# Seven block products for ten pairs of gate blocks, and 32x32 turns that go through device memory, in a two-layer gated mixer trunk

## What is computed

```
h = rms_norm(x, pre_g);  proj = h @ w_in           # w_in: 2048 x 24576
q_a k_a v_a z_a | u b c z | q_r k_r v_r z_r | g_a g_c g_r = split(proj)
o_a = dilated_attention(q_a, k_a, v_a) * silu(z_a) # 12 heads x 128
o_c = b * causal_conv3(c * u) * silu(z)            # 1536 channels
o_r = retention(rotary(q_r), rotary(k_r), v_r) * silu(z_r)
merged = sigmoid(g_a)*(o_a @ w_a) + sigmoid(g_c)*(o_c @ w_c) + sigmoid(g_r)*(o_r @ w_r)
x = x + rms_norm(merged @ w_out, post_g)
```

## Time and profile before

| | us |
|---|---|
| median of three runs (2746.15 to 2746.77) | 2746.62 |
| profiled execution, from first to last instruction | 2743.0 |
| time outside that span | 3.6 |
| PE busy | 2732.6 |
| DVE busy | 1924.2 |
| ACT busy | 1222.0 |
| POOL busy | 27.5 |

### The profile page before, as it was taken

One profiled execution on the slowest core, in us unless ns is written; L12 is line 12 of the kernel. 1 busy time (PEld: TensorE's weight loads), 2 busy tenths in 40 slices (PEclk: granted clock), 3 DMA queues, 4 the chain that ended last, 5 costly groups with the idle time before them and its releaser, 6 DMA issues.

```text
span 2743.0 us, 30433 instructions
## 1 busy us (share of the span) xinstructions
PE 2732.6 (100%) x12264; PEld 2268.3 (83%) x12264; DVE 1924.2 (70%) x2558; ACT 1222.0 (45%) x1404; POOL 27.5 (1%) x35
## 2 busy tenths in 40 slices
PE   9999999999999999999999999999999999999998
PEld 7888888888888888888878888888888888888887
DVE  6788744777655898858567887457676558977584
ACT  6454544444443334444454545444444433434443
POOL 0000000000000000000000000000000000000000
PEclk9999999999999999999999999999999999999999
DMA  9555566565555555556575555555656565555563
GB/s 333 184 172 196 170 200 194 190 199 188 196 195 190 184 184 176 182 195 221 180 238 175 184 190 179 197 188 187 202 193 198 188 197 177 191 171 182 199 215 138
DMA packets 264732, 529.10 MB, mean 193 GB/s; under 512 B 8464, under 2 KB 8848, under 8 KB 264336
## 3 DMA queue, kind: packets, MB, share of 16 engines
q1 hardware_dynamic: 260976, 517.50, 57.4%
q10 hardware_dynamic: 2608, 4.78, 0.5%
q0 software_dynamic: 1008, 4.87, 0.5%
HBM read 522.94 MB, written 4.19 MB: 192 GB/s over the span
## 4 chain that ended last, share of the span: by engine, by line
PE 99%; DVE 0%; issue 0%; ACT 0%; DVEq 0%; POOL 0%; POOLq 0%
PE ps L651 32%; PE ps L652 32%; PE ps L653 32%; PE ps L586 0%; PE ps L606 0%; PE ps L604 0%; PE ps L603 0%; PE ps L582 0%; PE ps L567 0%; PE ps L587 0%; PE ps L581 0%; PE ps L669 0%; DVE gates L1183 0%; DVE w_trail L913 0%; DVEq L231 0%
## 5 line engine op out<-in xcount | busy, mean ns | idle before, releaser
L913 DVE TENSOR_TENSOR w_trail<-raw,w_lead 128x1024 fp32r<-128x1024 f32 x973 | 1188.7, 1225 | 763.8 <-ACT w_lead L723 754.4
L723 ACT ACTIVATE w_lead<-raw 128x1024 fp32r<-128x1024 f32 x973 | 1028.3, 1060 | 1394.1 <-PE ps L653 1387.3
L651 PE MATMUL ps<-w_lead,hT_lead 128*128 128x512 f32 x3328 | 1299.1, 390 | 0.8 <-issue 0.4
L653 PE MATMUL ps<-w_lead,hT_trail 128*128 128x512 f32 x3328 | 1295.2, 389 | 0.0
L652 PE MATMUL ps<-w_trail,hT_lead 128*128 128x512 f32 x3328 | 1295.1, 389 | 0.0
L651 PEld LDWEIGHTS ps<-w_lead,hT_lead 128*128 128x128 f32 x3328 | 625.0, 188 | 131.1 <-issue 2.2
L653 PEld LDWEIGHTS ps<-w_lead,hT_trail 128*128 128x128 f32 x3328 | 624.9, 188 | 130.0
L652 PEld LDWEIGHTS ps<-w_trail,hT_lead 128*128 128x128 f32 x3328 | 625.1, 188 | 128.4
L651 PE MATMUL ps<-w_lead,oT_lead 128*128 128x512 f32 x576 | 224.3, 389 | 0.0
L653 PE MATMUL ps<-w_lead,oT_trail 128*128 128x512 f32 x576 | 224.1, 389 | 0.0
L652 PE MATMUL ps<-w_trail,oT_lead 128*128 128x512 f32 x576 | 224.1, 389 | 0.0
(11 more groups left out here) (102 smaller groups left out, 781.7 us busy)
## 6 DMA issues: line engine op xcount, KB each, us to landing
raw<-w_in SPq DMA_DIRECT2D x381, 1024.0 KB, 5.1
raw<-w_out SPq DMA_DIRECT2D x32, 1024.0 KB, 5.0
raw<-w_branch_a SPq DMA_DIRECT2D x24, 1024.0 KB, 5.0
raw<-w_branch_c SPq DMA_DIRECT2D x24, 1024.0 KB, 5.0
raw<-w_branch_r SPq DMA_DIRECT2D x24, 1024.0 KB, 5.0
raw<-w_in SPq DMA_DIRECT2D x5, 512.0 KB, 5.0
gates<-x SPq DMA_DIRECT2D x4, 512.0 KB, 13.5
post_gain<-post_norm_g POOLq DMA_DIRECT2D x2, 1024.0 KB, 8.2
```

The lines of the kernel that those rows point to most:

```text
L651: pe.matmul(acc, lead[:, k, tok(t)], wl, start=(k == 0), stop=False)
L653: last = pe.matmul(acc, trail[:, k, tok(t)], wl, start=False, stop=(k == BLOCKS[n][2] - 1))
L723: act.activation(w_lead[:, h % SPLIT_SLOTS, :], raw[:, i % RAW_SLOTS, part:part + HALF * COLS], ACT.Copy).then_inc(lead_ready, 1)
L913: dve.tensor_tensor(w_trail[:, s, :], raw[:, i % RAW_SLOTS, part:part + HALF * COLS], w_lead[:, s, :].bitcast(F32), ALU.subtract).then_inc ...
```

## The change

**Turns.** The evictions now write q, k, z and the conv product in an order cut by 32 columns (`quads`), and PE reads the weights of those blocks in that order (`columns`: runs of 32 elements). ACT sends the tile to a buffer in device memory (`send_away`, 512 KB) and starts four transfers that bring it back with its 32-row bands exchanged (`bring_back`, rows of 1 KB). Then two DVE transposes of all 128 partitions finish it (`turn_back`) where there were sixteen of 32 partitions. `probs` is turned as before. There are 24 such trips in a layer.

**Pairs.** For ten pairs of gate blocks (in each layer attention 2+3, conv 0+1 and 2+3, retention 0+1 and 2+3) the first eight slices of both blocks are multiplied as a 2x2 by 2x2 block product with seven products of four slices and one token tile instead of eight. A pair runs as 22 units in the order `PAIR_ORDER`; 14 of them are product units of 6 matmuls, 8 are plain units of 12. Four products need sums of weights: POOL adds a chunk from device memory onto a chunk in its raw slot by an accumulating transfer (`chunk_sum`, 1 MiB) once that chunk has been split for its earlier use. The left sides are formed once a layer (`form_work`). `p1`, `p6` and `p7` add up in one side bank; ACT copies the bank out after each (`pair_copy`), DVE forms differences (`pair_rest_of`), adds them at eviction, and ACT applies the sigmoid behind that.

**Conv's tail** runs gates 0 and 1, branches 0 and 1, gates 2 and 3, branches 2 and 3. `RAW_SLOTS` becomes 5, with slots given out by last use; `post_gain` shares the storage of `v_sb` and `q_sb`; constants are laid out for the new column order.

```
+PAIRED_GATES = {"attention": (2,), "conv": (0, 2), "retention": (0, 2)}
+PAIR_ORDER = ("p1", "q3", 0, 0, "q5", 0, 0, "p2", "p6", "p7", 1, 1, "q4", 1, 1)
+PAIR_CHUNK_ORDER = ((0, 0), (1, 1), (0, 2), (0, 3), (0, 1), (1, 2), (1, 3))
+SUM_AFTER = {"q5": "p1", "p7": "q3", "p6": "q5", "q4": "p6"}
...
 ACT_DUE = due({
-    "attention": [("exp", 4 * B + 1), ("out", 6 * B + 1)],
-    "conv": [("out", 4 * B + 6)],
-    "retention": [("square", 4 * B + 3), ("out", 5 * B + 3)]}, AHEAD)
+    "attention": [("q_away", 2 * B - 1), ("q_back", 2 * B + 1), ("k_away", 3 * B - 1), ("k_back", 3 * B + 1),
+                  ("exp", 4 * B + 1), ("z_away", 5 * B + 4), ("z_back", 5 * B + 6), ("out", 6 * B + 1)],
+    "conv": [("prod_away", 2 * B + 1), ("prod_back", 2 * B + 3), ("z_away", 4 * B + 1), ("z_back", 4 * B + 3),
+             ("out", 4 * B + 6)],
+    "retention": [("q_away", 2 * B + 1), ("q_back", 2 * B + 3), ("k_away", 3 * B + 1), ("k_back", 3 * B + 3),
+                  ("square", 4 * B + 3), ("z_away", 4 * B + 6), ("z_back", 4 * B + 8), ("out", 5 * B + 3)]}, AHEAD)
...
+PAIR_COPY_DUE = {UNIT_AT[kind, n, 1] + AHEAD: (kind, n) for n in PAIRS for kind in ("p1", "p6", "p7")}
+PAIR_REST_DUE = {UNIT_AT[kind, n, 1] + AHEAD + 1: (kind, n) for n in PAIRS for kind in ("p6", "p7")}
...
+            def chunk_sum(l, what, n):
...
+                wait(*split_done(l, UNIT_AT[SUM_AFTER[what], n, CHUNK // HALF - 1]))
+                at = l * tiles + row * CHUNK
+                pool.dma_start(raw[:, slot, :].rearrange("p (k n) -> p k n", k=CHUNK),
+                               weights[name][:, at:at + CHUNK, col:col + COLS],
+                               accum_op=ALU.add).then_inc(summed[SUMMED_FOR[what]], 16)
...
+            def product(l, h, what, n, part):
...
+                if part == 0:
+                    if what == "p1":
+                        pe.wait_ge(*side_bank_free(l, p_step))
+                    elif what == "q5":
+                        pe.wait_ge(*side_bank_free(l, q_step))
+                        pe.wait_ge(form_trail, TILES * (l + 1))
+                    elif what in ("p6", "p7"):
+                        pe.wait_ge(pair_copied, 2 * pair_no(l, n) + 1 + (what == "p7"))
+                    elif what == "q3":
+                        pe.wait_ge(*bank_free(l, n + 1))
...
+                elif kind == "gate" and n in PAIR_OF:
+                    act.wait_ge(*moved_out(l, n))
+                    for t in range(TILES):
+                        cols = slice(COLS * j, COLS * (j + 1))
+                        act.activation(gates[:, t, cols], gates[:, t, cols], ACT.Sigmoid,
+                                       scale=x_rstd[:, t:t + 1]).then_inc(gate_ready, 1)
...
+            def bring_back(l, what, mixer, g):
...
+                act.wait_ge(away[to], 16 * trips(l, to, mixer, g))
+                rows = bounce[to].rearrange("(i b) (j c) -> j b i c", i=QUADS, j=QUADS)
+                for j in range(QUADS):
+                    act.dma_start(tile[SQ * j:SQ * (j + 1), :].rearrange("b (i c) -> b i c", i=QUADS),
+                                  rows[j]).then_inc(back[to], 16)
...
+            def turn_back(l, what, mixer, g):
...
+                dve.wait_ge(back[to], 16 * QUADS * trips(l, to, mixer, g))
+                squares = src.rearrange("p t c -> p (t c)").rearrange("p (i t h a) -> p t h i a", i=QUADS, t=TILES, h=HPB)
+                for t in range(TILES):
+                    last = dve.transpose(dst[:, :, tok(t)].rearrange("p h (i b) -> p h i b", i=QUADS), squares[:, t])
+                last.then_inc(done, 1)
```

More of the change, by code:

```diff
@@ L33 @@
 HALF = 2
-RAW_SLOTS = 4
+RAW_SLOTS = 5
 SPLIT_SLOTS = 4
@@ L75, in layer_blocks @@
                                ("mix", mixer, role, g)))
[L76 to L79, removed]
+        for kind, j in TAIL[mixer]:
+            if kind == "gate":
+                blocks.append(("w_in", COLS * (GATES_AT + OUT_BLOCKS * b + j), KT, ("gate", mixer, "", j)))
+            else:
+                blocks.append((mixer, COLS * j, KT_MIX, ("branch", mixer, "", j)))
     for j in range(OUT_BLOCKS):
@@ L187 @@
 ACT_DUE = due({
-    "attention": [("exp", 4 * B + 1), ("out", 6 * B + 1)],
-    "conv": [("out", 4 * B + 6)],
-    "retention": [("square", 4 * B + 3), ("out", 5 * B + 3)]}, AHEAD)
-DVE_DUE = due({
[L192 to L195, removed]
-    "retention": pieces("q", 2 * B) + pieces("k", 3 * B) + [("scores", 3 * B + 7), ("values", 4 * B + 3),
-                  ("norm", 4 * B + 4), ("gate", 4 * B + 5)] + pieces("z", 4 * B + 6) + [("out", 5 * B + 4)]}, AHEAD)
@@ new lines @@
+DVE_DUE = due({
+    "attention": [("q", 2 * B + 4), ("k", 3 * B + 4), ("scores", 4 * B), ("sums", 4 * B + 2)]
+                 + pieces("probs", 4 * B + 3) + [("values", 5 * B + 3), ("z", 6 * B), ("out", 6 * B + 2)],
+    "conv": [("prod", 2 * B + 6), ("conv0", 2 * B + 6), ("conv1", 2 * B + 7), ("conv2", 3 * B),
+             ("gate", 4 * B), ("z", 4 * B + 6), ("product", 4 * B + 6), ("out", 4 * B + 7)],
+    "retention": [("q", 2 * B + 6), ("k", 3 * B + 5), ("scores", 3 * B + 7), ("values", 4 * B + 3),
+                  ("norm", 4 * B + 4), ("gate", 4 * B + 5), ("z", 5 * B + 2), ("out", 5 * B + 4)]}, AHEAD)
@@ L215, with side_list @@
 MERGE_TRAIL_DUE = {h + 1: j for h, j in MERGE_LEAD_DUE.items()}
-RESIDUAL_DUE = FIRST_HALF[MERGE_BLOCK0 + OUT_BLOCKS] + AHEAD + 1
+RESIDUAL_DUE = FIRST_HALF[BLOCK_NO["out", "", "", 0]] + AHEAD + 1
+def side_list():
+    steps = [("x", t, j) for t, j in X_ORDER]
+    for h, (kind, n, at) in enumerate(UNITS):
+        if kind in ("p1", "q5") and at == 0:
+            steps.append(("pair", kind, n))
+        for what, mixer, g in PE_DUE.get(h, []):
+            steps += [(what, mixer, g, i) for i in range(HPB if what == "scores" else HPB // 2)]
+        if h in MERGE_DUE:
+            steps += [("merge", MERGE_DUE[h], t) for t in range(TILES)]
+    return steps
+SIDE_LIST = side_list()
+SIDE_STEPS = len(SIDE_LIST)
+STEP = {key: m for m, key in enumerate(SIDE_LIST)}
+READY_STEPS = [sum(key[0] != "pair" for key in SIDE_LIST[:m]) for m in range(SIDE_STEPS + 1)]
+FORMS = {"p6": 0, "q3": 1, "p7": 2, "q5": 3}
+FORM_STEPS = ("whole", "sums", "lead", "trail")
+FORMS_FROM = 2 * B
+PAIR_COPY_DUE = {UNIT_AT[kind, n, 1] + AHEAD: (kind, n) for n in PAIRS for kind in ("p1", "p6", "p7")}
+PAIR_REST_DUE = {UNIT_AT[kind, n, 1] + AHEAD + 1: (kind, n) for n in PAIRS for kind in ("p6", "p7")}
+SUM_DUE = {UNIT_AT[before, n, 1]: (kind, n) for n in PAIRS for kind, before in SUM_AFTER.items()}
+NORM_DUE = {h: g for h, dues in DVE_DUE.items() for what, _mixer, g in dues if what == "norm"}
 def build(nc, x, xT, w_in, w_attention, w_conv, w_retention, w_out, post_g, params, consts, out):
@@ L709, in split_lead @@
             def split_lead(l, h):
-                i, part = chunk_of(l, h)
+                what, n, _at = place(l, h)
+                i, part = chunk_and_part(l, h)
                 part = part * HALF * COLS
```

547 lines of the change are left out of this document (394 added, 153 removed).

## The result

| | before | after |
|---|---|---|
| median, us | 2746.39 (2745.60 to 2746.77, 4 runs) | 2910.43 (2908.12 to 2911.67, 4 runs) |
| profiled span, us | 2743.0 | 2906.3 |
| PE busy / not busy in the span, us | 2732.6 / 10.4 | 2780.7 / 125.6 |
| mean granted clock | 0.999 | 0.981 |

What follows compares the result with a forecast made beforehand. PE, busy 100% of the span, was taken as the bound: 2746.6 - 27.2 (fewer matmuls) + 40 (new waits) = 2759 us, if the sums land in time. The forecast's own range was 2748 to 2770, for all runs 2731 to 2803.

Steps and rivals of the forecast that it cites:

- The matmuls: In the ten pairs, seven products for eight: 120 fewer matmuls at 0.2267 us, -27.2 us.
- The six new waits: PE waiting on ACT and DVE hand-offs in the pairs: 20.0 us a layer, +40 us in both.
- waits for ACT's copy: p7 waits for ACT's copy of p6: 0.92 us in every pair, 4.05 in conv 0+1, 3.8 in retention 0+1.
- q3 of retention 2+3: Retention's second pair: queued tail work and gate evictions make PE start q3 3.6 us late, 4.3 with unit 4's split.
- p1 of retention 0+1: Retention's first pair: p1 needs the first score's side bank, which DVE drains late; PE starts 2.05 us late.
- q3 of conv's pairs: q3 waits for the bank of block n-1: 1.12 us in conv 2+3, 1.26 in conv 0+1.
- Rival A: Pairs with a mixer's tail: hand-offs stay local, waits only 8.1 us a layer, 2736 us; chance 0.33.
- Moving operand in runs of 32: 5760 matmuls of the cut blocks read so: taken as 0, upper end 5 ns each, 29 us.
- Rival C: Cut blocks: the cut read costs PE 5 ns a matmul, 2788 us; chance 0.04.
- Do they?: Sums landing in time: L (release to landing) taken as 8 to 9 us; up to 10 costs nothing.
- Rival B: Sums come late: at L = 11, p6 and q4 wait, 44 us over ten pairs, 2803 us; chance 0.22.
- Among plain units these hide: Turns through memory: ACT's issues for the trips, five of about 0.49 us each, cost PE nothing among plain units.

Runs made afterwards that it cites:

- two_no_sums: two_pairs without its eight adding transfers, so its paired gates are not the reference's: 2740.32 us, ratio 0.998.
- no_sums: The changed kernel without the forty adding transfers and the waits for them, so products use unsummed weights: 2809.04 us, ratio 1.0228.
- write_cut: turns_only with the moving operand read in order and the result written to PSUM in runs of 32: 2746.33 us, ratio 1.0001.
- plain_sums: The changed kernel with POOL's adding transfers replaced by plain loads that overwrite the chunk, same places and waits: 2817.03 us, ratio 1.0256.
- two_pairs: The changed kernel with doubled POOL descriptor space, cut on the write side, p7 behind the second gate's ordinary halves, and only attention's pair: 2754.28 us.
- ring4096: The changed kernel with 4096 instead of 2048 bytes per partition for POOL's descriptors, cosine table narrowed to make room: 2862.40 us, ratio 1.0425.
- light_loads: ring4096 with SP's loads of the pairs' chunks cut to half their bytes, adding transfers whole: 2856.91 us, ratio 1.0404.
- turns_only: The changed kernel with no gate pairs; turns through memory, cut column order, five raw slots and conv's tail by twos remain: 2785.42 us, ratio 1.0142.
- late_p7: ring4096 with p7's sum released one half unit after p6's instead of some 8 us before it: 2889.00 us, ratio 1.052.

## Why the prediction was right or wrong

**The matmuls: right.** 120 fewer, and where nothing hinders, each is worth 0.2267 us (two_no_sums: 24 fewer, 5.4 us worked out, 2745.72 - 2740.32 = 5.4 measured).

**The six new waits: right, as far as they went.** Forecast 40 us of idle; no_sums has 36.5 more than before. The waits for ACT's copy were to be 21.2 in all (six of 0.92, two of 4.05, two of 3.8) and are 19.4 there (0.69, 3.50 and 4.16 each); q3 of retention 2+3 was to wait 3.6 and waits 3.5; p1 of retention 0+1 2.05, and waits 1.6; q3 of conv's pairs 1.12 and 1.26, and waits 0.89 and 0.97. Only attention's q3 (0.7) does not wait at all. Following each engine's queue gave these. Rival A, for which the prediction gave a third, is answered too: the queued waits did reach PE.

**The low clock: a term that was missing.** The sum priced idle at its own length. In no_sums 36.5 us of idle went with 17.2 more, in the changed kernel 115 with 36.5: a third to a half on top. After a long wait PE ran at the lower of its two levels (0.50 granted at 850 us). The trace of before had one such stretch only, at its end: PE's last matmul starts at 2735.46, and the clock granted from 2740 us on is 0.50. It is a term that any forecast of new waits has to bound. At that rate 40 us of idle cost 19 more, and the forecast would have been 2778.

**"Moving operand in runs of 32": wrong, +38.8 us against 0.** The reason given, that all present forms have one spacing, compared forms that all read in order, so it said nothing about this one. The two ends were 0 and 29, and the range of an unmeasured cost should not have ended at an assumed fiftieth of a matmul. Rival C had the mechanism, with 6.7 ns measured for its 5, and a chance of only 0.04, for which no row spoke. The Trainium skill (Advanced Engine Details and Errata, Memory Cachelines) was read there as making such runs free; on the read the measurement says otherwise. Of PSUM the same section says that "any non-contiguous AP significantly slows down matmuls"; here runs of 32 columns written to PSUM cost nothing (write_cut, 0.2267), so trusting it would have kept the permutation on the side where it costs.

**"Do they?", the landing of the sums: wrong, 101 us against 0.** Two errors in one step. The size: 10.0 us in the median where I took 8 to 9 from POOL's loads of `post_gain`. That this was near is luck: those loads spread one row of gains over all partitions, and plain loads of weights from POOL land in 5.6 (plain_sums), so no row of before stood for a sum. Even so, by the formula itself L = 10 leaves no room, and two_pairs, with the doubled space, idles 4 us more in each pair than two_no_sums. The mechanism: L was counted "from release to landing", each sum by itself. But p7's sum stands in POOL's queue ahead of p6's, and with the space of 2048 POOL starts the next only when the one ahead has about landed: in conv's second pair p6's sum waited 9.2 us between its release and its issue. Half of the 101 us, 48, came back with the doubled space (ring4096). Rival B named the step but only its size; it priced 44 us for L = 11, and by its engine time argument, which light_loads refutes for the most part (5.5 us). The rule that it cited, that an adding transfer reads its destination as well (the Trainium skill, DMA: Bandwidth & Descriptors, Rules for kernel authors), agrees with the packets, 22128 for the 11888 of plain loads.

**"Among plain units these hide": right** for the turns (turns_only idles 1 us more than before).

**The range.** B and C were taken as alternatives to each other, each on top of 2759. They are separate costs that add: 2759 + 44 + 29 is 2832 even at my sizes, 29 above the upper end. Of the clauses that would make me wrong, "sums land in more than 10 us" stood exactly at what came.

## What to carry to other kernels

When a step adds several unmeasured things, the upper end is their sum, not the worst of them; and of each new form of operand or transfer, ask what row shows *that* form. For a transfer, the landing counts from its issue; before that comes all that stands ahead of it in the queue of the engine that issues it. Where PE is the bound and never idle, a saving of matmuls is real but small (2.7 us a pair here), so it pays only in places where the other engines have room, and with the extra work on the engine that has it: DVE's adds at 1.2 us kept about half of it (3.2 us of 5.4 in attention's two pairs, 5.1 of 10.9 in four), transfers that add and POOL's adds at 3.0 us lost it more than twice over (14.0 us for 5.4).

## What the runs showed of the hardware

- A 1 MiB adding transfer from POOL: 1.29 us to issue and 10.0 to land, at least 8.4 (8.3 in ring4096); the same as a plain load 0.75 and 5.6. It takes 1.9 times the packets.
- How many such transfers are under way hangs on the space for descriptors: at 2048 POOL stood idle in front of 14 of the 40 with nothing else to wait for (129.9 us), at 4096 in front of 4 (30.4 us), or of 8 when the sums are asked for in another order (63.7 us, late_p7). At 4096 two can overlap, and the slowest took 19.0 us.
- A matmul of 512 columns whose moving operand is read in runs of 32 or 16 columns has a spacing of 0.231 to 0.233 us for 0.2267; in runs of 64 there is no loss, and written to PSUM in runs of 32 none either.
- An add of 1024 float32 columns takes DVE 1.22 us and POOL 3.03; a DVE split beside POOL's took 2.1 us for 1.23.
- After 8.4 us of idle PE's matmuls stood 0.427 us apart at a granted clock of 0.50; at 1.00 it is 0.227.
